# Routed experts: one run of ten turnings per unit, up weights copied 2048 columns at a time, one down piece copied by GpSimd

## The reference

```
xb  = t_pad[rows]
hid = jax.nn.silu(xb @ w_gate[e]) * (xb @ w_up[e])     # 1024 -> 256
y   = hid @ w_down[e]                                  # 256 -> 1024
```

## Time and profile before

| | |
|---|---|
| three runs | 3912.29, 3918.79, 3921.03 us |
| median | 3918.79 us |
| span of the profiled execution | 3909.9 us |
| routed experts stage in it | about 3386 to 3909.9 us |
| TensorE busy, whole program | 3620.3 us (93%) |
| VectorE busy | 2604.2 us (67%) |
| ScalarE busy | 1556.1 us (40%) |
| GpSimd busy | 683.5 us (17%) |

### The profile page before, as it was taken

How to read it: one execution, slowest core, us unless ns; L and a number is a source line. 1 busy time by engine, 2 the same in 40 slices (tenths; PEclk the granted TensorE clock), 3 DMA queues, 4 the chain that set the end, 5 groups by cost and what they waited for, 6 DMA issues and landing times. The chain is left out here.

```text
span 3909.9 us, 65811 instructions
## 1 busy us (share of the span) xinstructions
PE 3620.3 (93%) x23087; PEld 2405.3 (62%) x23088; DVE 2604.2 (67%) x4816; ACT 1556.1 (40%) x3431; POOL 683.5 (17%) x802
## 2 busy tenths in 40 slices
PE   6999999799898977999999899998999999699998
PEld 4667777455584435878786677765666555344444
DVE  1567666565587866887876487785333576678886
ACT  1112221355563432212121467664333223367775
POOL 0000000100172320212221010110000132322222
PEclk8999999899999988999999999998999999799999
DMA  6122222222525568666665221224240143598974
GB/s 249 68 92 86 73 90 88 74 82 81 149 100 195 188 248 315 213 225 207 229 203 144 82 65 61 65 64 129 65 134 17 39 151 119 222 334 268 322 247 98
DMA packets 226958, 574.60 MB, mean 147 GB/s; under 512 B 27898, under 2 KB 100730, under 8 KB 210862
## 3 DMA queue, kind: packets, MB, share of 16 engines
q1 hardware_dynamic: 177486, 395.90, 28.9%
q0 software_dynamic: 49248, 175.79, 15.3%
HBM read 433.57 MB, written 137.93 MB: 146 GB/s over the span
## 5 line engine op out<-in xcount | busy, mean ns | idle before, releaser
L4948 DVE COPY moe_bu<-moe_wu 128x1024 f32 x480 | 298.7, 698 | 38.9 <-issue 17.2
L4835 PE MATMUL moe_psU<-moe_bu,shared_weights 128*32 128x256 f32 x3840 | 295.5, 383 | 1.1 <-issue 1.1
L4835 PE MATMUL moe_psU<-moe_wu,shared_weights 128*32 x1280 | 293.6, 382 | 2.1 <-DVE moe_bu L4948 1.4
L4166 PE MATMUL inp_psU<-shared_weights,inp_w 128*128 128x256 f32 x1024 | 232.0, 382 | 4.4 <-ACT inp_fm L3906 2.7
L4166 PEld LDWEIGHTS inp_psU<-shared_weights,inp_w 128*128 128x128 f32 x1024 | 195.5, 192 | 37.4 <-issue 9.2
L4904 ACT ACTIVATE moe_bd<-moe_wd 128x1024 f32 x200 | 198.0, 1049 | 29.0 <-PE moe_psD L4857 29.0
L4835 PEld LDWEIGHTS moe_psU<-moe_wu,shared_weights 128*32 128x32 f32 x1280 | 134.8, 110 | 111.5 <-issue 12.2
L1058 PE MATMUL inp_psU<-inp_hT,inp_w 128*128 128x256 f32 x896 | 196.6, 380 | 0.6 <-DVE inp_tm L852 0.6
L1058 PEld LDWEIGHTS inp_psU<-inp_hT,inp_w 128*128 128x128 f32 x896 | 169.6, 190 | 23.1 <-issue 1.0
L1555 DVE TENSOR_SCALAR_CACHE_REDUCE att_junk<-att_psS,att_snk 128x640 f32<-128x640 f32 x128 | 108.1, 882 | 110.0 <-PE att_psS L1474 110.0
L4857 PE MATMUL moe_psD<-moe_bd,moe_hT 128*32 128x512 f32 x960 | 153.8, 596 | 0.0
(11 more groups left out here) (807 smaller groups left out, 8772.1 us busy)
## 6 DMA issues: line engine op xcount, KB each, us to landing
moe_wu<-in_w_up SPq DMA_DIRECT2D x32, 2048.0 KB, 9.5
moe_d_w<-in_w_down SPq DMA_DIRECT2D x16, 2048.0 KB, 13.4
moe_wd<-in_w_down SPq DMA_DIRECT2D x32, 1024.0 KB, 11.5
moe_u_w<-in_w_up SPq DMA_DIRECT2D x15, 2048.0 KB, 13.8
mod_w<-in_w_ada SPq DMA_DIRECT2D x24, 1024.0 KB, 11.7
inp_mod_w<-in_w_mod SPq DMA_DIRECT2D x16, 1024.0 KB, 5.6
xn<-out_xn POOLq DMA_DIRECT2D x32, 512.0 KB, 4.8
shared_weights<-in_w_gate SPq DMA_DIRECT2D x8, 2048.0 KB, 9.2
```

The lines of the kernel that those rows point to most:

```text
L4166: mm = pe.matmul(psU[:, m % 2, u % 2 * G:(u % 2 + 1) * G], w[:, k, TM2_W + u * P:TM2_W + (u + 1) * P], hT[:, par, k, :], start=(k == 0), s ...
L4835: mm = pe.matmul(psU[c, f, 0:2 * P], xT[:, p, k, c], w, start=(k == 0), stop=(k == KD - 1), tile_position=(0, g * LOT))
L4948: ins = dve.tensor_copy(bu[:, g - 1, f, c, :].rearrange("p k n -> p (k n)").unsqueeze(1), wu[:, bass.ds(slots[g - 1], 1), f, c, :].rearran ...
```

## The change

TensorE does all four lifts of a unit first, then one run of ten transposes (hidden 0, the eight of unit u+1, hidden 1), then both lowers. VectorE copies the up weights in six pieces of 2048 columns (f whole) in place of twelve of 1024; `up_copied` counts two per unit. `copy_last` moves from VectorE to GpSimd, between `gather(u+2)` and `put(u-1)`, behind waits for `unit_ready` and `lowered`. On VectorE `give(u-1)` goes ahead of `mix(u, 0)`. On ScalarE both `bd` copies of half f=1 follow `silu(0)`, and the order of the rest follows TensorE's.

```diff
+            def copy_last(u):                                  # GpSimd
+                slot = slot_of(experts_of(pool, u), LOTS - 1)
+                pool.wait_ge(unit_ready, u + 1)
+                if late(u, 1):
+                    pool.wait_ge(lowered, u)
+                pool.tensor_copy(bd[:, LOTS - 2, FB - 1, :].unsqueeze(1), wd[:, bass.ds(slot, 1), FB - 1, :]).then_inc(last_copied, 1)
             def body(u, j):
                 if not isinstance(u, int) or u + XB < NU:
                     gather(u + XB, j % XB)
+                copy_last(u)
                 if late(u, 1):
                     put(u - 1, (j - 1) % 2)
...
             def body(u, j):                                    # TensorE
-                if follows(u):
-                    turn(u + 1, 1 - p, 0)
-                lift(u, p, slot, 0, 0)
-                lift(u, p, slot, 0, 1)
-                lift(u, p, slot, 1, 0)
-                turn_hidden(u, 0)
-                lift(u, p, slot, 1, 1)
-                lower(u, slot, 0)
+                for f in range(FB):
+                    for q in range(2):
+                        lift(u, p, slot, f, q)
+                turn_hidden(u, 0)
                 if follows(u):
-                    turn(u + 1, 1 - p, 1)
-                lower(u, slot, 1)
+                    for q in range(2):
+                        turn(u + 1, 1 - p, q)
+                turn_hidden(u, 1)
+                for f in range(FB):
+                    lower(u, slot, f)
...
+                silu(u, 0)                                     # ScalarE
                 copy_down(slots[0], 1, 1)
-                silu(u, 0)
+                copy_down(slots[1], 1, 2).then_inc(down_copied, 1)
+                silu(u, 1)
+                keep_hidden(u, 0)
                 if follows(u):
                     evacuate(u + 1, 1 - p, 0)
-                keep_hidden(u, 0)
-                silu(u, 1)
-                copy_down(slots[1], 1, 2).then_inc(down_copied, 1)
                 keep_hidden(u, 1)
...
-            def copy_up(slots, f, q):                          # VectorE
+            def copy_up(slots, f):
                 for g in range(1, LOTS):
-                    c = slice(4 * q, 4 * q + 4)
-                    ins = dve.tensor_copy(bu[:, g - 1, f, c, :]...
+                    ins = dve.tensor_copy(bu[:, g - 1, f, :, :]...
                 ins.then_inc(up_copied, 1)
...
-                mix(u, 0)
                 if late(u, 1):
                     give(u - 1, (j - 1) % 2)
-                copy_last(slot_of(here, LOTS - 1))
+                mix(u, 0)
                 mix(u, 1)
```

More of the change, by code:

```diff
@@ L4826, in lift @@
             def lift(u, p, slot, f, q):
-                pe.wait_ge(up_copied, u * 4 + (2 * f + q + 1))
-                pe.wait_ge(xT_ready, u * 2 + (q + 1))
+                if q == 0:
+                    pe.wait_ge(up_copied, u * 2 + (f + 1))
+                if f == 0:
+                    pe.wait_ge(xT_ready, u * 2 + (q + 1))
                 if q == 0 and late(u, 1):
@@ L4943, in give @@
                                              op0=ALU.mult, op1=ALU.mult).then_inc(y_ready, 1)
-            def copy_up(slots, f, q):
+            def copy_up(slots, f):
                 for g in range(1, LOTS):
-                    c = slice(4 * q, 4 * q + 4)
-                    ins = dve.tensor_copy(bu[:, g - 1, f, c, :].rearrange("p k n -> p (k n)").unsqueeze(1),
-                                          wu[:, bass.ds(slots[g - 1], 1), f, c, :].rearrange("p a k n -> p a (k n)"))
+                    ins = dve.tensor_copy(bu[:, g - 1, f, :, :].rearrange("p k n -> p (k n)").unsqueeze(1),
+                                          wu[:, bass.ds(slots[g - 1], 1), f, :, :].rearrange("p a k n -> p a (k n)"))
                 ins.then_inc(up_copied, 1)
@@ L4954, in copy_all_up @@
                 for f in range(FB):
[L4955 to L4959, removed]
+                    copy_up(slots, f)
             def mix(u, f):
@@ L4974, in body @@
             def body(u, j):
-                here = experts_of(dve, u)
                 if follows(u):
                     experts = experts_of(dve, u + 1)
-                mix(u, 0)
                 if late(u, 1):
                     give(u - 1, (j - 1) % 2)
-                copy_last(slot_of(here, LOTS - 1))
+                mix(u, 0)
                 mix(u, 1)
```

## The result

The changed kernel took 3939.82 us (median of 4 runs, 3936.57 to 3943.61) against 3919.05 before (4 runs, 3912.29 to 3921.03). The ratio is 1.0057, 95% interval 1.0045 to 1.0069: slower by 21 us. The forecast was 3936, 17 us slower, by a wait of TensorE for the up copies, which GpSimd's copy delays.

The account below looks back on a forecast made before the run. TensorE was taken to set the pace at 12.46 us a unit; after the change, waiting for up copies, +23 us over 39 units, less 3.5 irregular, 1.0 and 1.1 at the ends: +17.4, median 3936, whole range 3908 to 3960.

Parts of the forecast that it names:

- What GpSimd's copy costs VectorE: Among VectorE's six up copies: GpSimd's down-piece copy of 1.03 us makes VectorE lose 0.93 us a unit.
- The reading of rows 8: VectorE's longest up copy, 867 ns against a median of 685, was taken as lengthened 0.18 by a GpSimd index copy.
- 0.16 that I charged to the index copies: In VectorE's up copies: GpSimd's two index copies cost 7.48 - 7.32 = 0.16 us, half in each triple.
- pair of the earlier trace: A GpSimd instruction overlapped a VectorE TENSOR_SCALAR by 0.56 us; it took 1.11 where the shortest takes 0.752, costing 0.36.
- d: VectorE's loss to GpSimd's down-piece copy in each unit: taken as 0.93 us, bounds nothing and 2.26.
- Copies of 2048: VectorE's up copies of twice the columns: 1.13 us each, the middle between 1.06 and 1.206.
- Ten transposes in one run: On TensorE, three runs of transposes, together 2.11 us, become one of 1.73; TensorE alone then needs 12.22 a unit.
- The f=0 lifts start at 5.31: not late: On TensorE: the first three up copies end at 5.09 us after the lifts' end, before the f=0 lifts start.
- side by side: Rival: GpSimd's copy costs VectorE nothing, TensorE's 12.22 us a unit bounds, 11.5 us faster, median 3907; chance 0.15.
- The unit: From one lifts' end to the next: 13.05 us against 12.46, with TensorE waiting 0.8 before the f=1 lifts.
- Irregular time: Of 7 us from loop-end gaps and late weights, half, 3.5 us, disappears under TensorE's waits; between 0 and 7.
- Ends: At the stage's two ends: unit 0 saves 1.0 us, the tail after the last lifts 1.1 us.

Follow-up runs that it names:

- after_put: The changed kernel with GpSimd's copy of the down piece moved behind put(u-1): 3916.5 us, ratio 1.0003 to the kernel before.
- run 23: Not a label of a run: the words are "costs the run 23 us", a time of 23 us.
- order_only: The changed kernel with only the new order kept, up pieces of 1024 columns and the down piece on VectorE again: 3896.5 us, ratio 0.9946 to the kernel before.
- small_pieces: The changed kernel with up pieces of 1024 columns again, GpSimd still copying the down piece: 3900.5 us, ratio 0.9962 to the kernel before.
- before_2048: The kernel before the change with up pieces of 2048 columns and nothing else: 3928.1 us, ratio 1.0033.
- back_on_vector: The changed kernel with the last down piece copied by VectorE again, between mix(0) and mix(1): 3916.5 us, ratio 0.9998 to the kernel before.
- copy_twice: The changed kernel with GpSimd's copy of the down piece done twice, one after the other: 3969.6 us, ratio 1.0136 to the kernel before.

## Why the prediction was right

The mechanism that decided the time held: VectorE's copies, made longer by GpSimd's, released the f=1 lifts too late. Around it several terms and one reading were off, in part against each other.

- *What GpSimd's copy costs VectorE*: 0.93 predicted, 0.84 measured, in three doses (none, one, two), and it vanishes when the copy lies elsewhere (after_put). That is shown. It also needed its place in the order: the same 0.84 costs the run 23 us with coarse pieces and 5 in the old order; with small ones (order_only to small_pieces) it is 4, and there the intervals overlap.
- *The reading of rows 8*: wrong. VectorE's longest copies, up to 867 ns, are not stretched by an index copy. The stretched one of the unit in the earlier trace rows is the sixth, and GpSimd's indirect DMA of the gathered rows ends inside it. In small_pieces the same copy is stretched though no GpSimd copy runs in it; the down piece starts only at its end (before: DMA, then VectorE's sixth copy; small_pieces: the same):

```profile
3582.73 1.25 POOL L4789 DMA_INDIRECT shared_rows<-xn,moe_at  x1 [0.79 <-POOL moe_at L4786]
3583.63 0.85 DVE L4948 COPY moe_bu<-moe_wu 128x1024 f32 x1
...
3612.81 1.26 POOL L4789 DMA_INDIRECT shared_rows<-xn,moe_at  x1 [0.79 <-POOL moe_at L4786]
3613.71 0.85 DVE L4954 COPY moe_bu<-moe_wu 128x1024 f32 x1
```

With pieces of 2048 columns no such stretch is seen (in before_2048 the longest copy takes 1241 ns against a median of 1220). So the 0.16 that I charged to the index copies is not theirs. The 0.54 of the earlier trace rows shows that GpSimd waits for a boundary, not that VectorE loses by it. What was left for a loss of VectorE was the pair of the earlier trace rows, and its 0.36 is measured against the shortest TENSOR_SCALAR; against the median, 929 ns, it is 0.18. That d came out within 0.09 is in part luck.

- *Copies of 2048*: 1.13 predicted, 1.14 measured.
- *Ten transposes in one run*: 1.73 predicted, 1.36 measured (3603.97 to 3605.33). The eight turnings take 0.88 (3604.25 to 3605.13), 0.11 each, where I had taken 0.145 from a run of four whose time held its exit as well. With the 0.14 of the change of unit gone too, TensorE alone needs 11.72 (order_only), not 12.22, so the order was worth 0.73 in a regular unit, three times what I gave it, and 0.53 on the mean.
- *"The f=0 lifts start at 5.31: not late"*: wrong, and by my own words a wait before the f=0 lifts was to count against the forecast. TensorE reached the f=0 lifts 4.82 after the lifts' end, not 5.31, and the third copy ended at 5.31 (3609.28), with the lifts starting 0.34 after that. It did no harm to the number: in the changed kernel the time of the unit is set by VectorE's chain to the f=1 lifts, whenever the f=0 lifts start. With GpSimd's copy gone it binds and makes the unit 12.29 in place of 11.72. The rival "side by side" had 12.22 there, near the measured 12.29 but for another reason.
- *The unit*: 13.05 predicted, 13.17 measured in the middle and 12.98 at the end of the stage. The sum by measured terms: 1.81 to the first copy, 7.75, 0.14 to the f=1 lifts, 3.48 for them: 13.18. The excess is in the 1.81 (1.62 before).
- *Irregular time*: I took 3.5 us off a rise of 23. The starts of the copies of unit 2 and of unit 40 are 3401.38 and 3882.57 before, 3408.20 and 3911.67 after: 12.66 and 13.25 a unit, 0.59 more, which times 39 is 23. By the first hidden transposes the mean goes from 12.63 to 13.24 and the regular unit from 12.45 to 13.17, so the irregular part falls from 7 us to about 3: the size of the term was near. But the weights did not all land less late, as I had argued: at the step to unit 35 the excess over a regular unit grew from 1.5 to 4.6 us. The rise of 23, where 19.5 was forecast, comes from a unit 0.12 longer than forecast, not from this term.
- *Ends*: the tail from the last lifts' end fell from 17.54 to 16.3, -1.3 for -1.1 predicted.

Span against span the difference is 29.4 us, more than the 21 between the medians. The routing stage ahead of the experts, which the change does not touch, ended 7.2 us later in this execution (VectorE's `row_table` copy of L4694 at 3387.08, before at 3379.84), and 29.4 - 7.2 = 22.2 is the stage's own. The profiled execution of before was thus among its fastest. For the changed kernel the execution took 3940.89 with a span of 3939.3, 1.6 around it; the 8.9 that I put between span and median was mostly this, and not an overhead.

Of the whole change, in regular units near 3600 us: the order -0.73 (12.45 to 11.72), the coarse pieces +0.57 (to 12.29), GpSimd's copy +0.88 (to 13.17, with the late `silu(1)`). On the mean of the 39 steps, which goes with the time: -0.53, +0.51 and +0.63, or -21, +20 and +25 us; the medians give -22, +20 and +23.

## What to carry to other kernels

Before work is handed from one engine to another, ask what the two share at that moment, not how idle the new one is: a copy on GpSimd stopped VectorE's copies for nearly its full length. A piece size is a latency: longer copies saved VectorE 0.57 us a unit and cost TensorE as much, as soon as the order left the copies on the critical path. And when edits come together, time them one by one: one of these three was worth 0.5% and the other two hid it.

## What the runs showed of the hardware that was not expected

- Eight transposes in a row follow each other every 0.11 us at 2.4 GHz; a run costs about 0.3 us more than its transposes at that rate (0.40 for one, 1.36 for ten).
- In the changed kernel `silu(1)` starts 0.31 us after the first hidden transpose in the middle of the stage (3604.40 and 3604.09) and 0.14 after it at the end (3910.30 and 3910.16); in back_on_vector, small_pieces, order_only and copy_twice it is 0.13 in the middle too, in after_put up to 0.2. It came again in the second execution (3600.93 and 3600.63). The cause is open.
- GpSimd took its turn at the next boundary between two back-to-back VectorE copies for all 39 down pieces of the changed kernel that met them; in small_pieces 8 of 39 ended one boundary later. VectorE then itself waited until GpSimd's copy was through.
- A VectorE copy of 1024 columns took 0.85 us in place of 0.68 when the gather's indirect DMA, begun 0.90 us before it, ended 0.36 us into it (before, small_pieces). Copies of 2048 columns were not stretched. The cause was not tested.
- After 6.2 us without work TensorE came back at a granted clock of 0.50 for about 4 us (back_on_vector); after 4.8 us it did so in order_only as well, with eight groups started 0.41 to 0.43 us apart; after 1.4 us it did not (before).
